# Opening stage of a two-block transformer kernel: normalization after the transposition, projections in one stage

## The chip, the core and the metric

The kernel runs on one core of a Trainium2 chip. The metric is the device time in microseconds of one execution. A core has five engines with their own instruction streams: TensorE (PE; PEld is its weight load), VectorE (DVE), ScalarE (ACT), GpSimd (POOL) and SyncE (SP), which here only issues DMAs. They meet through semaphores.

## What is computed

The reference is a block with a gated mixer (differential attention, banded attention) and a mixture of experts, followed by a second block. The change touches only its beginning:

```python
h = layer_norm(x, ln_in_g, ln_in_b)      # x: (1, 512, 1024); (x - mu) * rsqrt(var + 1e-5) * g + b
proj = h @ w_in
qa, ka, va = ...                         # the first three groups of 512 columns of proj
out_a = diff_attention(qa, ka, va, lam, lam_init, subln_w)   # 4 heads; p[0] - lam * p[1] of two softmaxes
...
h = layer_norm(DEEPNORM_ALPHA * h + m, ln1_g, ln1_b)         # the normalized h is needed again here
```

## The kernel before

`program` writes one core's streams stage by stage; a `Stage` ends when all engines have joined (the line of these joins is L80 in the profile). Matrices are multiplied as pairs of fp32r parts: an operand is split in an upper part (ScalarE casts it) and a lower part (`split_lower`, L141, raw minus upper), and `split_product` (L134 to L136) issues three matmuls: upper by upper, upper by lower, lower by upper. `k.x_parts` holds the transposed activations, eight chunks of 128 features by 512 rows. `k.ahead` is a buffer for weights that are loaded ahead (its lower part lies over it), `k.v_upper` that of their upper part.

The opening has three stages.

- `setup_stage` ("setup"): SyncE loads x in two halves (`x_in`), gain and shift spread to all partitions, the value weights (`load_ahead`, 2 MB), and stores two small rows of relative biases. ScalarE issues the constants and small loads, makes the four bias tables `alibi` (L354), and takes the root (L205). VectorE takes the statistics of the four row tiles (L118), the mean and variance (L199, L201), the inverse with one correction (L210 to L221), and normalizes each row tile in two passes: L227 ((x - mean) * gain) and L230 (times factor, plus shift), each 128x1024. TensorE only makes one small product (L365).
- `layer_norm_stage` ("ln0", with `done=NT`: rows are already normalized): SyncE writes the spread table `z_band` and loads the mask and the gain and shift of the next normalization; TensorE transposes x (L300: 32 of 128x128, four to a bank); ScalarE casts each chunk (L289), VectorE takes its lower part from the bank.
- `first_attention_stage` "diff" calls `heads_stage` (`early` is true: values are projected here). Unit u is one of four heads; its query and key weights lie in `raw0` for even u and over `k.ahead` for odd u. ScalarE casts the value weights (L789), VectorE splits them in four parts, TensorE projects values to banks 3 to 6, in groups of two chunks, once a part is split; then unit 0's queries and keys to banks 7 and 2 (`FIRST_PROJECTED`), with weights loaded from 35.87 (L867), cast (L761) and split on GpSimd. ScalarE copies queries (L783), VectorE keys (L810). From the first score (L454) on, `attention_pe` weaves the products of unit u + 1 (`projection`) between the steps of unit u. The second unit's weights can only be loaded when the value products have ended, since they lie over the value weights.

What sets the order is each engine's program order and its waits; there is no planner.

## Time and profile before

| what | us |
|---|---|
| median of 3 runs (lowest, highest) | 2136.57 (2133.35, 2140.83) |
| the profiled execution's own time | 2135.08 |
| its span in the trace | 2133.2 |
| TensorE busy in the span | 1939.7 (91%), 10052 matmuls |
| VectorE busy | 1602.6 (75%) |
| ScalarE busy | 1226.0 (57%) |
| GpSimd busy | 296.6 (14%) |

The page has the shares of the whole span. A busy share is a mean over stages with different limits, so the order of time within a stage is what tells what waits for what. Stretches are given from the start of the span. The granted clock (PEclk) is the share of TensorE's full 2.4 GHz; it has two levels, 1.00 and 0.50.

### The profile page before, as it was taken

What the parts mean: (1) busy time and instruction counts of PE and PEld (TensorE: products, weight loads), DVE (VectorE), ACT (ScalarE), POOL (GpSimd) and SP (SyncE); (2) the same over time, 40 slices, a digit from 0 to 9 for tenths busy, and PEclk for the clock granted to TensorE, in tenths of its full rate; (3) what the DMA queues carried; (4) which work ended last, traced back from release to release, by engine and by line L of the source; (5) the groups of instructions that cost most, each with busy time, mean ns of one, the idle gap of its engine ahead of it and who ended that gap; (6) DMA issues with size and microseconds to landing.
All of it is one profiled execution on the core that took longest, in us unless ns stands there. A gap on an engine that the chain in (4) does not pass through costs nothing. (4 is left out here: it accounts for less than half of the span.)

```text
span 2133.2 us, 28805 instructions
## 1 busy us (share of the span) xinstructions
PE 1939.7 (91%) x10052; PEld 1553.1 (73%) x10052; DVE 1602.6 (75%) x1819; ACT 1226.0 (57%) x1311; POOL 296.6 (14%) x172
## 2 busy tenths in 40 slices
PE   4988999974999999999999999999999388989998
PEld 3766678753788888888888888888888276576876
DVE  5362441457899999999999999999998544634786
ACT  3343532323677777777777777777777134643551
POOL 0202044101021212120212121211111000000000
PEclk9999999986999999999999999999999688999999
DMA  6222143445899999999999999999999362011122
GB/s 207 60 79 80 30 104 104 161 139 232 311 372 393 372 394 365 398 376 393 372 390 374 389 373 394 371 393 371 396 375 349 88 154 60 16 36 59 54 67 79
DMA packets 201613, 518.95 MB, mean 243 GB/s; under 512 B 21975, under 2 KB 81503, under 8 KB 201197
## 3 DMA queue, kind: packets, MB, share of 16 engines
q1 hardware_dynamic: 191212, 482.68, 60.9%
q0 software_dynamic: 9504, 34.61, 6.3%
q8 instruction: 41, 0.67, 0.1%
q10 hardware_dynamic: 832, 0.80, 0.1%
q14 instruction: 24, 0.19, 0.0%
HBM read 494.41 MB, written 29.41 MB: 246 GB/s over the span
## 5 line engine op out<-in xcount | busy, mean ns | idle before, releaser
L1770 ACT CAST moe_upper<-piece 128x2048 fp32r<-128x2048 f32 x384 | 734.2, 1914 | 282.5 <-PE bank L1702 268.0
L1850 DVE TENSOR_TENSOR piece_lower<-piece,moe_upper 128x2048 fp32r<-128x2048 f32 x384 | 870.2, 2286 | 28.4 <-ACT moe_upper L1770 28.4
L1700 PE MATMUL bank<-moe_upper,x_hi 128*128 128x512 f32 x1536 | 620.5, 404 | 2.5 <-DVE x_hi L1844 2.5
L1702 PE MATMUL bank<-moe_upper,x_hi 128*128 128x512 f32 x1536 | 605.8, 394 | 0.0
L1701 PE MATMUL bank<-piece_lower,x_hi 128*128 128x512 f32 x1536 | 601.2, 391 | 0.0
L1700 PEld LDWEIGHTS bank<-moe_upper,x_hi 128*128 128x128 f32 x1536 | 289.9, 189 | 67.8 <-DVE piece_lower L1850 2.9
L1701 PEld LDWEIGHTS bank<-piece_lower,x_hi 128*128 128x128 f32 x1536 | 290.1, 189 | 63.0
L1702 PEld LDWEIGHTS bank<-moe_upper,x_hi 128*128 128x128 f32 x1536 | 289.5, 188 | 62.8
L1654 POOL DMA_INDIRECT mixed<-moe_y,moe_dst x32 | 104.7, 3272 | 27.5 <-issue 27.5
L136 PE MATMUL bank<-x_hi,ahead_lower 128*128 128x512 f32 x256 | 102.0, 398 | 0.0
L1652 POOL COPY moe_dst<-row 128x1 uint32 (+1 forms) x32 | 7.0, 218 | 621.0 <-ACT moe_y L1759 621.0
L1644 POOL COPY moe_tok<-token 128x1 uint32 (+1 forms) x34 | 24.8, 729 | 335.1 <-DMA mixed<-moe_y,moe_dst 273.7
L1137 DVE TENSOR_TENSOR merge_tmp<-merge_sig,bank 128x512 f32<-128x512 f32 x8 | 5.5, 688 | 81.7 <-PE bank L136 81.4
L1646 POOL DMA_INDIRECT ahead<-h,moe_tok x34 | 61.7, 1813 | 32.5 <-issue 32.5
L300 PE MATMUL bank<-const,xs 128*128 128x128 f32 x96 | 18.0, 359 | 44.3 <-DVE xs L230 24.3
L136 PEld LDWEIGHTS bank<-x_hi,ahead_lower 128*128 128x128 f32 x256 | 49.4, 193 | 11.0
L135 PE MATMUL bank<-ahead_lower,x_hi 128*128 128x512 f32 (+1 forms) x140 | 55.4, 395 | 0.0
L134 PE MATMUL bank<-x_hi,merge_upper 128*128 128x512 f32 x128 | 50.4, 394 | 4.1 <-DVE ahead_lower L141 4.1
L1839 DVE TENSOR_TENSOR moe_a<-moe_u,moe_sg 128x512 f32<-128x512 f32 x64 | 44.3, 693 | 10.6 <-issue 10.2
L300 PEld LDWEIGHTS bank<-const,xs 128*128 128x128 f32 x96 | 15.8, 190 | 48.6 <-DVE xs L230 45.2
L135 PE MATMUL bank<-x_lo,merge_upper 128*128 128x512 f32 x128 | 50.5, 395 | 0.0
L1833 DVE SCALAR_TENSOR_TENSOR moe_u<-moe_u,moe_g 128x512 f32<-128x512 f32 x64 | 44.3, 693 | 5.9
(570 smaller groups left out, 3031.5 us busy)
## 6 DMA issues: line engine op xcount, KB each, us to landing
piece<-in_w_exp_in_dram SPq DMA_DIRECT2D x256, 1024.0 KB, 7.6
piece<-in_w_exp_out_dram SPq DMA_DIRECT2D x128, 1024.0 KB, 9.5
ahead<-in_w_in_dram SPq DMA_DIRECT2D x19, 512.0 KB, 4.1
ahead<-in_w_in_dram SPq DMA_DIRECT2D x3, 2048.0 KB, 9.3
ahead<-in_w_in_dram SPq DMA_DIRECT2D x4, 1536.0 KB, 7.0
merge_raw<-in_w_in_dram SPq DMA_DIRECT2D x8, 512.0 KB, 5.4
ahead<-in_w_out_dram SPq DMA_DIRECT2D x2, 2048.0 KB, 8.0
out_w<-in_w_out_dram SPq DMA_DIRECT2D x2, 2048.0 KB, 8.3
```

Source lines behind the costliest of these rows:

```text
L134: nc.tensor.matmul(out, lhs.hi, rhs.hi, start=start, stop=False)
L135: nc.tensor.matmul(out, lhs.hi, rhs.lo, start=False, stop=False)
L136: return nc.tensor.matmul(out, lhs.lo, rhs.hi, start=False, stop=stop)
L1646: nc.gpsimd.indirect_dma_start(out=rows_in[p][:, :], out_offset=None, in_=k.h1[:, :], in_offset=bass.IndirectOffsetOnAxis(ap=tok[:, p:p + ...
L1654: nc.gpsimd.indirect_dma_start(out=k.mixed[:, :], out_offset=bass.IndirectOffsetOnAxis(ap=dst[:, 0:1], axis=0), in_=y[:, :], in_offset=Non ...
L1700: nc.tensor.matmul(to, hi[:, f, :], upper[u][:, t, cols], start=f == 0 and not biased, stop=False)
L1701: nc.tensor.matmul(to, hi[:, f, :], lower[s][:, t, cols], start=False, stop=False)
L1702: done = nc.tensor.matmul(to, lo[:, f, :], upper[u][:, t, cols], start=False, stop=f == NK - 1)
L1770: nc.scalar.copy(upper[h % SPLIT][:, :, :], ring[s][:, :, :]).then_inc(hi_ready, 1)
L1833: nc.vector.scalar_tensor_tensor(out=u2[half][:, :], in0=u2[half][:, :], scalar=1.0, in1=g2[half][:, :], op0=ALU.add, op1=ALU.mult)
L1839: nc.vector.tensor_tensor(a2[half][:, :], u2[half][:, :], sg2[half][:, :], ALU.mult) .then_inc(a_ready, 1)
L1850: nc.vector.tensor_tensor(lower[s][:, :, :], ring[s][:, :, :], upper[h % SPLIT][:, :, :].bitcast(F32), ALU.subtract).then_inc(lo_ready, 1)
```

## The change

The three pieces (setup, first normalization, and value and first unit's projection) become one stage, `opening_stage`; `FirstNorm` and `setup_stage` go.

- x is loaded in four tiles. Gain and shift are also loaded as 16 rows of 128, transposed by one TensorE instruction and copied to `cols`, a column for each chunk.
- A row tile is only centered and scaled by its own factor: tiles 0 and 2 on VectorE (`tensor_scalar`), 1 and 3 on ScalarE (`Identity` with scale and offset). Gain and shift are applied after the transposition, where they are one number a partition, as VectorE takes the chunk from its bank to `full`, a ring of three; ScalarE then casts from `full`, VectorE subtracts.
- The split of the value weights is woven into this loop. TensorE turns chunks 0 to 3 (banks 0, 1, 2, 7), then alternates two chunks' value products with turning two further chunks, and adds unit 0's queries and keys. Unit 0's weights are loaded at the start of the program, and split on VectorE.
- The row tiles of x get gain and shift afterwards, in two passes each (`scaled_row`): three before VectorE waits for the value products, the fourth at the end.
- The second unit's weights are loaded, cast and split in this stage too, behind the value products (`v_ps`); the next normalization's gain and shift are loaded last (`scaled`, NT + 1). The write of `z_band` and the load of the mask stand ahead of these.
- The mask of `alibi` and the weight `neg_lam` are made on VectorE in the attention stage, behind the copy of the keys (`differential_weight`). `heads_stage` skips for units 0 and 1 what is done already (`opened`, `split`).
- The new stage's semaphores are kept and freed with those of the experts' stages.

```diff
-class FirstNorm:
...
-def setup_stage(nc, k, A, alibi):
...
+OPEN_TURNED, OPEN_VALUES = (0, 1, 2, 7), (3, 4, 5, 6)
+
+
+def opening_stage(nc, k, A, alibi, oa_first):
+
+    w_in = A["w_in"][0]
+    (raw, lower, upper), v_w = oa_first, Split(k.v_upper[:, :, :], k.ahead_lower[:, :, :])
+    unit_w = [Split(upper[:, NK * n:NK * n + NK, :], lower[:, NK * n:NK * n + NK, :]) for n in range(2)]
+    next_raw, next_lower, next_upper = second_unit(k, 2 * NK)
+    with Stage(nc, "setup", k.spent) as st:
...
         @block.sync
         def _(sp):
-            for h in range(2):
-                sp.dma_start(k.x[:, 2 * h:2 * h + 2, :], A["x"][0, 2 * h * P:2 * (h + 1) * P, :]
-                             .rearrange("(i p) n -> p i n", p=P)).then_inc(x_in[h], 16)
+            for i in range(NT):
+                sp.dma_start(k.x[:, i, :], A["x"][0, i * P:(i + 1) * P, :]).then_inc(x_in[i], 16)
+            for n, v in enumerate(("ln_in_g", "ln_in_b")):
+                sp.dma_start(rows_in[NK * n:NK * n + NK, :], A[v].rearrange("(c p) -> c p", p=P)).then_inc(rows_landed, 16)
+            for h in range(4):
+                sp.dma_start(k.ahead[:, 2 * h:2 * h + 2, :], column_tiles(w_in, 2 * WA, 512)[:, 2 * h:2 * h + 2, :])\
+                    .then_inc(v_in[h], 16)
+            for n in range(2):
+                sp.dma_start(raw[:, NK * n:NK * n + NK, :], column_tiles(w_in, n * WA)).then_inc(unit_in, 16)
             load_norm(sp, k, A["ln_in_g"], A["ln_in_b"])
-            for h in range(2):
-                sp.wait_ge(x_in[h], 16)
-            load_ahead(sp, k, column_tiles(A["w_in"][0], 2 * WA, 512))
             sp.wait_ge(band_ready, 1)
             sp.dma_start(k.band_row, band_row[:, :]).then_inc(k.row_stored, 16)
             sp.wait_ge(t5_ready, 1)
             sp.dma_start(k.t5_row, t5_row[:, :]).then_inc(k.row_stored, 16)
             sp.wait_ge(k.row_stored, 32)
+            spread_row(sp, k.z_band, k.band_row, k.band_stored)
+            sp.dma_start(k.hg_mask[:, :], A["c_mask"]).then_inc(k.mask_in, 16)
+            sp.wait_ge(v_ps, NT)
+            for n in range(2):
+                sp.dma_start(next_raw[:, NK * n:NK * n + NK, :], column_tiles(w_in, n * WA + P)).then_inc(next_in, 16)
+            sp.wait_ge(scaled, NT + 1)
+            load_norm(sp, k, A["ln1_g"][0], A["ln1_b"][0])
 
         @block.scalar
         def _(act):
-            act.dma_start(k.const[:, :], A["c_f32"]).then_inc(const_in, 16)
             act.dma_start(rb[:, :], A["rel_bias"][0]).then_inc(rb_in, 16)
             act.dma_start(onehot[:, :], A["c_onehot"]).then_inc(t5_in, 16)
             act.dma_start(table[:, :], A["rel_bias_2"]).then_inc(t5_in, 16)
+            act.dma_start(k.const[:, :], A["c_f32"]).then_inc(const_in, 16)
             for n, v in enumerate(("lambda_q1", "lambda_k1", "lambda_q2", "lambda_k2")):
                 act.dma_start(lv[:, n, :], row_broadcast(A[v][0])).then_inc(lam_in, 16)
-            act.wait_ge(const_in, 16)
+            act.wait_ge(t5_ps, 1)
+            nc.scalar.copy(t5_row[:, 0:512], k.bank[OPEN_VALUES[0]][0:6, :])
+            act.drain().then_inc(t5_ready, 1)
+            act.wait_ge(cols_ps, 1)
+            nc.scalar.copy(cols[:, :], k.bank[OPEN_VALUES[1]][:, 0:2 * NK]).then_inc(cols_ready, 1)
+
+            def values_upper(h):
+                act.wait_ge(v_in[h], 16)
+                part = slice(2 * h, 2 * h + 2)
+                nc.scalar.copy(k.v_upper[:, part, :], k.ahead[:, part, :]).then_inc(v_hi, 1)
+
+            act.wait_ge(var_ready, 1)
+            norm.deviation(0, NT).then_inc(std_ready, 1)
+            values_upper(0)
+            act.wait_ge(scaled, 1)
+            for i in (1, 3):
+                nc.scalar.activation(k.x[:, i, :], k.x[:, i, :], ACT.Identity, scale=norm.r[:, i:i + 1],
+                                     bias=offset[:, i:i + 1]).then_inc(normed, 1)
+            for c in range(NK):
+                act.wait_ge(taken, c + 1)
+                nc.scalar.copy(k.x_parts.hi[:, c, :], full[:, c % 3, :]).then_inc(hi_copied, 1)
+                if c % 2 == 0 and c < 6:
+                    values_upper(c // 2 + 1)
+            act.wait_ge(unit_in, 32)
+            for n in range(2):
+                part = slice(NK * n, NK * n + NK)
+                nc.scalar.copy(upper[:, part, :], raw[:, part, :]).then_inc(unit_hi, 1)
             for h in range(4):
                 nc.scalar.activation(alibi[:, h, :], k.const[:, C_DIST:C_DIST + S], ACT.Copy,
                                      scale=2.0 ** (-2 * (h + 1)))
-            act.wait_ge(t5_ps, 1)
-            nc.scalar.copy(t5_row[:, 0:512], k.bank[0][0:6, :])
-            act.drain().then_inc(t5_ready, 1)
-            act.wait_ge(var_ready, 1)
-            rows.deviation(0, NT).then_inc(std_ready, 1)
+            act.wait_ge(v_ps, NT)
+            for i in (0, 2):
+                nc.scalar.copy(k.v[:, i, :], k.bank[OPEN_VALUES[i]][:, :])
+            act.wait_ge(next_in, 32)
+            for n in range(2):
+                part = slice(NK * n, NK * n + NK)
+                nc.scalar.copy(next_upper[:, part, :], next_raw[:, part, :]).then_inc(next_hi, 1)
+            act.wait_ge(k.lam_ready, 1)
+            nc.scalar.activation(k.lam_exp[:, :], k.lam_sum[:, :], ACT.Exp)
 
         @block.tensor
         def _(pe):
             pe.wait_ge(t5_in, 32)
-            nc.tensor.matmul(k.bank[0][0:6, :], table[:, :], onehot[:, :], start=True, stop=True).then_inc(t5_ps, 1)
+            nc.tensor.matmul(k.bank[OPEN_VALUES[0]][0:6, :], table[:, :], onehot[:, :], start=True, stop=True)\
+                .then_inc(t5_ps, 1)
+            pe.wait_ge(const_in, 16)
+            pe.wait_ge(rows_landed, 32)
+            nc.tensor.transpose(k.bank[OPEN_VALUES[1]][:, 0:2 * NK], rows_in[:, :], k.ident[0:2 * NK, 0:2 * NK])\
+                .then_inc(cols_ps, 1)
+
+            def turn(c):
+                if c >= 4:
+                    pe.wait_ge(taken, c - 3)
+                for i in range(NT):
+                    last = nc.tensor.transpose(k.bank[OPEN_TURNED[c % 4]][:, i * P:(i + 1) * P],
+                                               k.x[:, i, c * P:(c + 1) * P], k.ident)
+                last.then_inc(transposed, 1)
+
+            pe.wait_ge(normed, NT)
+            for c in range(4):
+                turn(c)
+            pe.wait_ge(t5_ready, 1)
+            pe.wait_ge(cols_ready, 1)
+            for h in range(4):
+                pe.wait_ge(v_lo, h + 1)
+                for c in (2 * h, 2 * h + 1):
+                    pe.wait_ge(copied, c + 1)
+                    for i in range(NT):
+                        last = split_product(nc, k.bank[OPEN_VALUES[i]][:, :], k.x_parts[:, c, i * P:(i + 1) * P],
+                                             v_w[:, c, :], c == 0, c == NK - 1)
+                        if c == NK - 1:
+                            last.then_inc(v_ps, 1)
+                if h < 2:
+                    turn(4 + 2 * h)
+                    turn(5 + 2 * h)
+            for n in range(2):
+                pe.wait_ge(unit_lo, n + 1)
+                for c in range(NK):
+                    split_product(nc, k.bank[FIRST_PROJECTED[n]][:, :], unit_w[n][:, c, :], k.x_parts[:, c, :],
+                                  c == 0, c == NK - 1)
...
             for i in range(NT):
-                dve.wait_ge(x_in[i // 2], 16)
+                dve.wait_ge(x_in[i], 16)
                 statistics(nc, k, i)
             dve.drain()
-            rows.variance(dve, 0, NT).then_inc(var_ready, 1)
+            norm.variance(dve, 0, NT).then_inc(var_ready, 1)
             dve.wait_ge(std_ready, 1)
-            rows.inverse(dve, 0, NT)
-            dve.wait_ge(gain_in, 16)
-            dve.wait_ge(shift_in, 16)
-            for i in range(NT):
-                rows.row(dve, i).then_inc(normed, 1)
+            norm.inverse(dve, 0, NT)
+            nc.vector.scalar_tensor_tensor(out=offset[:, :], in0=norm.mv[:, :, 0], scalar=-1.0, in1=norm.r[:, :],
+                                           op0=ALU.mult, op1=ALU.mult).then_inc(scaled, 1)
+            for i in (0, 2):
+                nc.vector.tensor_scalar(k.x[:, i, :], k.x[:, i, :], norm.mv[:, i, 0:1], norm.r[:, i:i + 1],
+                                        ALU.subtract, ALU.mult).then_inc(normed, 1)
+            dve.wait_ge(cols_ready, 1)
+            for t in range(NK + 1):
+                if t < NK:
+                    dve.wait_ge(transposed, t + 1)
+                    if t >= 3:
+                        dve.wait_ge(copied, t - 2)
+                    nc.vector.tensor_scalar(full[:, t % 3, :], k.bank[OPEN_TURNED[t % 4]][:, :], cols[:, t:t + 1],
+                                            cols[:, NK + t:NK + t + 1], ALU.mult, ALU.add).then_inc(taken, 1)
+                if t % 2 == 0 and t < NK:
+                    part = slice(t, t + 2)
+                    dve.wait_ge(v_hi, t // 2 + 1)
+                    split_lower(nc.vector, k.ahead[:, part, :], k.v_upper[:, part, :],
+                                v_w.lo[:, part, :]).then_inc(v_lo, 1)
+                c = t - 1
+                if c >= 0:
+                    dve.wait_ge(hi_copied, c + 1)
+                    split_lower(nc.vector, full[:, c % 3, :], k.x_parts.hi[:, c, :], k.x_parts.lo[:, c, :])\
+                        .then_inc(copied, 1)
+            for n in range(2):
+                part = slice(NK * n, NK * n + NK)
+                dve.wait_ge(unit_hi, n + 1)
+                split_lower(nc.vector, raw[:, part, :], upper[:, part, :], lower[:, part, :]).then_inc(unit_lo, 1)
             dve.wait_ge(lam_in, 64)
             nc.vector.tensor_tensor(lp[:, 0, :], lv[:, 0, :], lv[:, 1, :], ALU.mult)
             nc.vector.tensor_tensor(lp[:, 1, :], lv[:, 2, :], lv[:, 3, :], ALU.mult)
             dve.drain()
-            nc.vector.tensor_reduce(k.lam_sum[:, :], lp[:, :, :], AX.X, ALU.add)
+            nc.vector.tensor_reduce(k.lam_sum[:, :], lp[:, :, :], AX.X, ALU.add).then_inc(k.lam_ready, 1)
+            dve.wait_ge(gain_in, 16)
+            dve.wait_ge(shift_in, 16)
+
+            def scaled_row(i):
+                nc.vector.tensor_tensor(k.x[:, i, :], k.x[:, i, :], k.gain[:, :], ALU.mult)
+                dve.drain()
+                nc.vector.tensor_tensor(k.x[:, i, :], k.x[:, i, :], k.shift[:, :], ALU.add).then_inc(scaled, 1)
+
+            for i in range(NT - 1):
+                scaled_row(i)
+            dve.wait_ge(v_ps, NT)
+            for i in (1, 3):
+                nc.vector.tensor_copy(k.v[:, i, :], k.bank[OPEN_VALUES[i]][:, :])
+            for n in range(2):
+                part = slice(NK * n, NK * n + NK)
+                dve.wait_ge(next_hi, n + 1)
+                split_lower(nc.vector, next_raw[:, part, :], next_upper[:, part, :], next_lower[:, part, :])
+            scaled_row(NT - 1)
+
+    k.norm.counted(normed=NT, std_ready=1)
+
+
+def second_unit(k, width):
+
+    return [x[:, 0:width // 4, :].rearrange("p a (b n) -> p (a b) n", n=P) for x in (k.ahead, k.ahead_lower, k.v_upper)]
+
+
+def differential_weight(nc, k, alibi, dve):
+
+    nc.vector.memset(alibi[0:HD, :, S - HD:S], NEG)
+    nc.vector.tensor_tensor(k.neg_lam[:, :], k.lam_exp[:, 1:2], k.lam_exp[:, 0:1], ALU.subtract)
+    dve.drain()
+    nc.vector.tensor_scalar(k.neg_lam[:, :], k.neg_lam[:, :], -LAM_INIT, None, ALU.add)
+    dve.drain()
...
+                opened=False, prepare=None):
+
+    early = values is not None and not projected_values and not opened
+    v_rows = range(2 if projected_values else 0, 0 if values is None or opened else NT)
...
+        split = 2 if opened else done
...
-            return k.bank[FIRST_BANK if u < done else FIRST_PROJECTED[n] if u == 0 else PROJECTED]
+            return k.bank[FIRST_BANK if u < done and keys is None else FIRST_PROJECTED[n] if u == 0 else PROJECTED]
...
-            for u in range(done, units):
+            for u in range(split, units):
...
+                if c == 0 and u >= split:
+                    pe.wait_ge(w_split, split0 + u * projections + n + 1)
...
-            if beside is None:
+            if beside is None and split < 2:
                 for n in range(projections):
                     upper_part(1, n)
...
+                if keys is not None and done <= u < units:
+                    dve.wait_ge(projected, projected0 + u * projections + projections)
                 if keys is not None and u < units:
-                    dve.wait_ge(projected, projected0 + u * projections + projections)
                     nc.vector.tensor_copy(keys[u % 2], place_of(u, 1)[:, :]).then_inc(evacuated, 1)
...
             next_keys(0)
+            if prepare is not None:
+                prepare(dve)
...
-                setup_stage(nc, k, A, table)
-                layer_norm_stage(nc, "ln0", k, k.x, x_t=k.x_parts, following=(A["ln1_g"][0], A["ln1_b"][0]),
-                                 first=FirstNorm(nc, k, A, table), done=NT)
+                (first_raw, first_lower), first_upper = overlaid(nc, s2, "first_raw", [P, 2 * NK, P]), s2.enter_context(
+                    nc.sbuf_tensor("first_upper", [P, 2 * NK, P], F32R))
+                first = first_raw, first_lower, first_upper
+                opening_stage(nc, k, A, table, first)
...
-                    lambda m: k.neg_lam[:, :] if m else None, differential_out, mixed=True, following=band_values)
+                    lambda m: k.neg_lam[:, :] if m else None, differential_out, mixed=True, following=band_values,
+                    first=first, opened=True, prepare=lambda dve: differential_weight(nc, k, table, dve))
```

## Rows read from the trace of the kernel before

**Rows 1.** Page, second part: busy tenths of TensorE in 40 slices

```profile
PE   4988999974999999999999999999999388989998
```

**Rows 2.** Stretches: length; PE, PEld, DVE, ACT, POOL busy (count); clock; DMA share, GB/s

```profile
27.00:31.00 4.00, 3.72 (x18) 3.75 (x19) 1.59 (x3) 3.17 (x6) 0.00 (x0) 1.00 0.69 246
31.00:33.00 2.00, 1.98 (x16) 1.61 (x14) 1.84 (x4) 1.94 (x4) 0.00 (x0) 1.00 1.02 256
33.00:36.00 3.00, 0.00 (x0) 0.00 (x0) 2.13 (x6) 0.76 (x3) 0.00 (x0) 1.00 0.90 273
...
38.20:41.40 3.20, 3.15 (x7) 2.51 (x8) 3.20 (x3) 1.58 (x2) 0.00 (x0) 0.50 1.04 386
41.40:61.60 20.20, 20.20 (x90) 16.73 (x89) 0.89 (x2) 3.17 (x4) 4.74 (x2) 1.00 0.16 39
```

**Rows 3.** Order of time, opening: start, us, engine, line, operation [idle before]

```profile
10.66 1.28 ACT L205 ACT_TABLE_LOAD   x1
11.23 2.47 DVE L118 BATCH_NORM_STATS2 stats<-xs 128x6 f32<-128x512 f32 x4 [0.86 <-DMA xs<-in_x_dram]
...
16.03 1.28 DVE L227 SCALAR_TENSOR_TENSOR xs<-xs,setup_mv,gain 128x1024 f32<-128x1024 f32 x1 [0.16 <-issue]
...
25.06 1.28 DVE L230 SCALAR_TENSOR_TENSOR xs<-xs,setup_r,shift 128x1024 f32<-128x1024 f32 x1
...
26.69 0.29 DVE L390 TENSOR_REDUCE lam_sum<-setup_lp 128x2 f32<-128x128 f32 x1
27.24 0.58 SPq L155 DMA_DIRECT2D z_band<-band_row  x1
```

**Rows 4.** Transpositions of the opening: in order of time, and by line (ns min/median/max)

```profile
27.28 5.70 PE L300 MATMUL bank<-const,xs 128*128 128x128 f32 x32 [17.32 <-PEq L80]
...
L300 PE MATMUL bank<-const,xs x32: 272/421/445, 27.3 to 32.7; 128*128 128x128 f32 x32
```

**Rows 5.** Order of time, from value products to first score

```profile
38.25 0.80 PE L134 MATMUL bank<-v_upper,x_hi 128*128 128x512 f32 x1 [5.27 <-DVE ahead_lower L141]
...
61.62 0.39 PE L134 MATMUL bank<-x_hi,diff_upper 128*128 128x512 f32 x1
...
72.70 0.69 DVE L810 COPY diff_heads_kt<-bank 128x512 f32<-128x512 f32 x1 [10.19 <-PE bank L136]
...
73.54 0.49 PE L454 MATMUL bank<-diff_heads_kt,diff_heads_q 64*128 64x128 f32 x4 [0.88 <-DVE diff_heads_kt L810]
```

**Rows 6.** Groups by line and shape: busy us, mean ns | idle before

```profile
L141 DVE TENSOR_TENSOR x_lo<-bank,x_hi 128x512 fp32r<-128x512 f32 x8 | 5.1, 687 | 2.6 <-ACT x_hi L289 2.6
L141 DVE TENSOR_TENSOR ahead_lower<-ahead,v_upper 128x1024 fp32r<-128x1024 f32 x4 | 4.6, 1220 | 1.8 <-ACT v_upper L789 1.8
L789 ACT CAST v_upper<-ahead 128x1024 fp32r<-128x1024 f32 x4 | 3.9, 1042 | 2.2 <-PEq L80 2.2
L1824 DVE TENSOR_SCALAR moe_g<-bank 128x512 f32<-128x512 f32 x64 | 41.0, 682 | 0.0
```

**Rows 7.** DMA: issues (KB each, median us to landing), then in order of time

```profile
z_band<-band_row SPq DMA_DIRECT2D x1, 2560.0 KB, 11.2
diff_raw<-in_w_in_dram SPq DMA_DIRECT2D x4, 512.0 KB, 6.5
ahead<-in_w_in_dram SPq DMA_DIRECT2D x2, 512.0 KB, 4.6
...
28.50 0.42 SPq L149 DMA_DIRECT2D gain<-in_ln_g_dram  x1
28.96 0.63 SPq L150 DMA_DIRECT2D shift<-in_ln_b_dram  x1
...
61.81 0.99 SPq L867 DMA_DIRECT2D ahead<-in_w_in_dram  x2
```

**Rows 8.** Stretches at the attention's end: length, TensorE busy (count), clock, DMA

```profile
133.61:137.02 3.41, 1.08 (x7) 1.00 0.00 0
137.02:140.44 3.42, 3.28 (x15) 0.50 0.02 5
```

More of the change, by code:

```diff
@@ L249, in _ @@
                 load_ahead(sp, k, ahead)
-            if first is not None:
-                first.spread(sp)
             if save is not None:
@@ L703, in _ @@
         def _(pool):
-            for u in range(done, units):
+            for u in range(split, units):
                 for n in range(projections):
```

64 lines of the change are left out of this document (24 added, 40 removed).

## The prediction

> **What bounds the kernel now.** I read the page first: TensorE is busy in nine tenths of the span, but the first of its 40 slices says 4 [rows 1]. The chain that ended last covers only the final few instructions, so it says nothing of the opening; I went on to the stretches (busy time and granted clock), then the order of time. The reader is to see a ladder in which each rung waits for the whole rung below. The statistics of the last two row tiles start at 11.23; the row scaling runs on VectorE alone from 16.03 to 26.34 (25.06 + 1.28); only after the stage joins at 27.24 does TensorE transpose, 27.28 to 32.98; then it stands 5.27 us until VectorE has split the first part of the value weights; the value products run 38.25 to 61.62, the first unit's 61.62 to 72.5, the keys are copied at 72.70, and the first score starts at 73.54 [rows 3 to 5]. In all of this TensorE's needed work is 5.7 + 23.4 + 10.9 = 40 us out of 73.5. Behind the first score the code of the change is the old one, and TensorE is full (every released unit has the next unit's products woven in). So the gain is the shift of the first score plus whatever clock is lost or won around it, and I price just that.
>
> **The change part by part.** Times are from the span's start.
>
> *Statistics.* Row tiles arrive one by one, in the same queue with the same bytes ahead of the last one, so the last lands near 11.2 as now; behind it stand two statistics instead of four. Four took 2.47 [rows 3], so they end at 12.5, not 13.7. From there to the first scaled row it takes 16.03 - 13.70 = 2.33 now. New on that way: ScalarE's copy of the gain and shift columns stands ahead of the root, with the small loads (queued behind x, about 11.6), one transposition (0.45), the copy (0.3) and then the root's table load of 1.28 [rows 3]: the root can't start before 13.6, 0.4 later than VectorE asks. Then the offset, 0.2: the factors are ready at 15.4.
>
> *Row scaling.* Eight VectorE passes of 1.28 leave the path; two rows stand on VectorE, two on ScalarE. For one ScalarE row the nearest is the 128x1024 cast, 1.04 [rows 6]: two end at 17.5. VectorE's two end there at the latest 0.5 later, if each costs a full 1.28. The function Identity has no row here: if it wanted a table load, 1.28 more; I take 0, since the casts after each of the loads in this opening needed none. The Trainium skill (ScalarE: Activation LUTs, section Table sets) says that identity sits in every set, which gives the same 0; no row shows it.
>
> *First product.* Turning chunk 0 is four transpositions. Those of now come at two speeds, 18 in 3.72 us and then 16 in 1.98 [rows 2]: 0.21 and 0.12 apart. Four at the slow pace and the end of the last: 18.5. VectorE then does in order the scaled eviction of chunk 0, the lower part of two value chunks, the eviction of chunk 1 and the lower part of chunk 0. An eviction with two factors has the row of 682, a lower part 687 for 512 columns and 1220 for 1024 [rows 6]; back to back each is some 0.07 shorter, so 3 x 0.62 + 1.16 and 0.2 of signalling: the first product starts at 21.8, now 38.25. Bounds: 20.9 (none of the small delays) to 24.0 (Identity load, VectorE rows at 1.28, 0.5 of later landing).
>
> *Value products.* The same 96 matmuls: 23.37 now, seven of them at half clock [rows 2, 5]. Woven in are the other 16 transpositions, 0.12 apart, 1.9, and 0.25 for the seams. VectorE has 2 x (0.62 + 0.62) + 1.16 = 3.6 us of work per pair of chunks where TensorE has 5.4 + 0.9, so it keeps up. The tight place is a wait: VectorE's eviction of chunk 4 waits for its turning, which TensorE does only after the first eight products' groups, and the lower part of chunk 3 is queued behind that eviction and a value split, 0.62 + 1.16 + 0.62 = 2.4 us, while TensorE has one more turning and chunk 2, 0.45 + 2.7: 0.7 of slack; the same again at chunks 5 and 6. Cost zero; if each VectorE step took 0.3 more, up to 0.5 in all. Products end at 21.8 + 23.4 + 1.9 + 0.25 = 47.3, now 61.62.
>
> *First unit.* Its weights land near 21; casts and splits (2 of 1.04, 2 of 1.22, on VectorE instead of GpSimd) end near 42, ahead of 47.3. Products 10.9, to 58.2. Hidden.
>
> *What ends the stage.* Now it is another chain. SyncE waits for the last value product, then loads the second unit: issue apart 0.5 and 4.6 to landing, 5.1 [rows 7]. ScalarE casts (1.04 to the first), VectorE splits two (after the first cast, 2.4), then the fourth row of x in two passes of 1.22, and SyncE, queued on that, issues two loads of 0.42 + 0.63 [rows 7]. 47.3 + 5.1 + 1.0 + 2.4 + 2.45 + 1.05 = 59.3. That is 1.1 behind TensorE. Joining the stage costs 0.26 (VectorE's last reduction ends 26.98, SyncE goes on at 27.24 [rows 3]) up to some 0.7: the keys are copied at 60.0 and the first score starts 0.84 later as now, at 60.85. The four tables, the lambda sums, three rows of x and the copies of the values lie in ScalarE's and VectorE's free time before 47.3 and during the second unit's load. The mask and lambda weight moved behind the keys copy take about 0.7 on VectorE and end as the first score is there. GpSimd's splits of two units go.
>
> *Sum.* 73.54 - 60.85 = 12.7 saved. *Clock.* TensorE then stands from 58.2 to 60.85. The granted clock stayed up over the 0.9 us at 72.6 and fell over 33 to 38; at the end of this same attention it fell to half after a stretch busy 1.08 of 3.4, whose longest stop was 2.0 [rows 2, 8]. 2.65 us is nearer to the rows that fell. A fall costs what the slow stretch at 38.2 cost, 7 x 0.2 and a part, 1.6, for the first unit's attention is full of woven products. I charge it: 11.1 saved.
>
> The profiled execution took 2135.08, which gives 2124.0; the median of the runs shown, 2136.57, lies 1.5 above it, and a median is what will be compared: **2125.5**.
>
> At the other end the rows speak of the clock too. 38.25 began slow after a stop; the first product at 21.8 follows 3.4 us of transpositions and a stop of 0.8. In the trace the clock rose under transpositions alone: they last from 272 to 445 ns with a median of 421, and the fast ones are the later [rows 2, 4]. So the 1.6 within 23.37 may go; I keep it, since the nearest row of a product behind a stop, 38.25, was slow. The Trainium skill (TensorE: Matmul & The Clock Gate, section Part 4: PE-mode transpose) says that transpositions don't count as work for the clock gate; the durations here speak against it. By the rule the slow start is certain, by the row it may be absent: 2125.5 or 2123.9.
>
> **The rivals.**
> *A, more is gained.* One of the two slow stretches is absent: 2125.5 - 1.6 = 2123.9; both: 2122.3. For it: the durations of the transpositions, and that 58.2 to 60.85 is half of the stop that surely cost. Against: the row at 137.
> *B, the entry and the exit are longer.* First product at the upper bound (+2.2) and the second unit's loads at the 6.5 of the first unit's row instead of 4.6 (+1.9) [rows 7]: 2125.5 + 4.1 = 2129.6. For it: 14 loads stand in SyncE's queue at once; against: in the trace loads landed in order of issue.
> *C, slower.* The clock stays at its lower level through both projections, because TensorE is fed in pieces: each product 0.427 instead of 0.227. With 137 products beyond the seven charged that is +27.4: 2153. It outweighs the gain from 56 such products on. For it: the tight hand-over at chunks 3 and 5; against: 3.6 of VectorE work to 6.3 of TensorE's per pair, so stops stay short.
> *D, no change.* The write of the spread table (2560 KB, 11.2 us [rows 7]) now stands ahead of the second unit's loads. If it is still moving at 47.3, they land up to 11.2 late and the stage ends that much later: 2136.7. It would have to be issued after 36; its small source rows are queued behind about 4.6 MB and I put its issue at 26.
>
> **How the numbers follow.** Forecast 0.45, A 0.30, B 0.15, C 0.05, D 0.05. The likeliest case is the forecast at 2125.5. The range is 2119.5 to 2131: A with both stretches and 3 us less for the spread of the runs (2133.35 to 2140.83), up to B and 1.4 more; it leaves out C and D and some of B. A measurement of this kernel can tell about 0.3%, 6.4 us, from no change, so faster means under 2130.2: forecast and A whole, B for the half, less a little for the spread, 0.82; the same 0.13; slower 0.05.
>
> **What would show it.** Per step: the first score near 60.9 (the sum), first value product near 21.8, last near 47.3 (feeding), root not before 13.6, no table load at the Identity rows, SyncE's last issues near 59 as the stage's end, clock rows of half near 22 to 25 and near 61 to 64. All later marks must stand the same distance from the first score as now; if not, the premise that only the opening moves is wrong. A first product later than 24 or a z-table write still open at 47 makes it B or D; halves of the clock through 22 to 58 make it C.

## The result, and the profile after

| | before | after |
|---|---|---|
| median of 6 runs (lowest, highest), us | 2136.99 (2133.35, 2140.83) | 2121.74 (2119.41, 2127.52) |
| profiled execution, span | 2133.2 | 2120.3 |
| its own time | 2135.08 | 2122.07 |

The ratio is 0.9929, 95% interval 0.9916 to 0.9943: 15.2 us faster by the medians (12.2 to 18.0 by the interval), 13.0 by the two profiled executions. The forecast was 2125.5.

TensorE's row in the page's 40 slices of the changed kernel, with the same columns as [rows 1]:

```profile
PE   7979899956999999999999999999999388989998
```

The first slice went from 4 to 7. Order of time of the changed kernel (start, us, engine, line, operation), the lines that answer to [rows 3 to 5]. First, the way to the first product:

```profile
10.26 1.29 DVE L118 BATCH_NORM_STATS2 stats<-xs 128x6 f32<-128x512 f32 x2 [1.38 <-DMA xs<-in_x_dram]
...
11.27 1.28 ACT L178 ACT_TABLE_LOAD   x1
12.56 0.20 ACT L178 ACTIVATE setup_std<-setup_ve 128x4 f32<-128x4 f32 x1
...
16.65 3.67 PE L396 MATMUL bank<-const,xs 128*128 128x128 f32 x16 [5.61 <-ACT xs L358]
21.29 0.76 PE L134 MATMUL bank<-v_upper,x_hi 128*128 128x512 f32 x1 [0.96 <-DVE x_lo L141]
```

Then the first unit's products, the last of them, SyncE's last loads, the copy of the keys and the first score:

```profile
46.84 0.39 PE L134 MATMUL bank<-x_hi,first_upper 128*128 128x512 f32 x1
...
57.49 0.39 PE L136 MATMUL bank<-x_hi,first_raw_lower 128*128 128x512 f32 x1
...
58.67 0.35 SPq L149 DMA_DIRECT2D gain<-in_ln_g_dram  x1
59.05 0.43 SPq L150 DMA_DIRECT2D shift<-in_ln_b_dram  x1
...
59.93 0.69 DVE L926 COPY diff_heads_kt<-bank 128x512 f32<-128x512 f32 x1 [1.29 <-PEq L80]
60.68 0.49 PE L567 MATMUL bank<-diff_heads_kt,diff_heads_q 64*128 64x128 f32 x4 [2.79 <-DVE diff_heads_kt L926]
```

The first score comes 73.54 - 60.68 = 12.86 earlier, and the span is 2133.2 - 2120.3 = 12.9 shorter: the whole difference of the two profiles stands before the first score. The first value product of the stage behind this attention has moved by the same 12.86 (before, then after):

```profile
146.46 0.79 PE L134 MATMUL bank<-v_upper,x_hi 128*128 128x512 f32 x1 [4.60 <-DVE ahead_lower L141]
```

```profile
133.60 0.79 PE L134 MATMUL bank<-v_upper,x_hi 128*128 128x512 f32 x1 [4.60 <-DVE ahead_lower L141]
```

If ScalarE's instructions of the two profiles are paired one by one, all from the first score to 150 stand 12.83 to 12.88 apart. Later the distance wanders between 12.0 and 15.0 and comes back to 13.0 at the end, so nothing lasting is won or lost there. Stretches of the opening, columns as in [rows 2]:

```profile
21.20:25.20 4.00, 3.91 (x9) 3.13 (x10) 3.71 (x5) 2.19 (x3) 0.00 (x0) 1.00 0.58 229
25.20:46.80 21.60, 21.60 (x104) 17.98 (x103) 14.49 (x19) 7.43 (x11) 0.00 (x0) 1.00 0.45 133
46.80:57.70 10.90, 10.90 (x49) 8.83 (x48) 8.92 (x10) 4.57 (x6) 0.00 (x0) 1.00 0.36 96
57.70:60.60 2.90, 0.18 (x1) 0.00 (x0) 1.61 (x2) 0.60 (x1) 0.00 (x0) 1.00 0.33 93
60.60:64.00 3.40, 3.32 (x16) 2.48 (x16) 0.96 (x8) 0.88 (x4) 0.00 (x0) 1.00 0.95 292
```

TensorE is full from 21.29 to 57.7: the ladder has become one woven stretch. The nine products in the first 4.0 us are slow ones. The granted clock reads 1.00 there only because its records in this trace begin at the first change, near 25.2; nine in 4.0 is 0.43 to 0.44 apiece, the pace of the 0.50 row in [rows 2]. The last two rows show what was charged and didn't come: TensorE stood 3.0 us, and behind it 16 matmuls went in 3.4 us at full clock.

### The profile page after: what moved, and what is told of

Same layout as the page of the kernel before. It is cut to its first block and busy times, and to the rows that moved or that the text cites. A ratio compares the mean times of both kernels' runs of the same rounds, so it can differ in the third digit from the quotient of the medians.

```text
span 2120.3 us, 28827 instructions
## 1 busy us (share of the span) xinstructions
PE 1940.5 (92%) x10053; PEld 1553.8 (73%) x10053; DVE 1614.4 (76%) x1834; ACT 1228.8 (58%) x1314; POOL 290.7 (14%) x168
## 5 line engine op out<-in xcount | busy, mean ns | idle before, releaser
L1763 POOL COPY moe_tok<-token 128x1 uint32 (+1 forms) x34 | 33.6, 988 | 333.6 <-DMA mixed<-moe_y,moe_dst 273.1
L1765 POOL DMA_INDIRECT ahead<-h,moe_tok x34 | 56.6, 1664 | 33.0 <-issue 33.0
L1958 DVE TENSOR_TENSOR moe_a<-moe_u,moe_sg 128x512 f32<-128x512 f32 x64 | 44.3, 693 | 10.6 <-issue 10.2
L1878 ACT ACTIVATE moe_y<-bank,slot_weight 128x512 f32<-128x512 f32 x64 | 40.2, 680 | 15.1 <-PE bank L1821 15.1
L1929 DVE TENSOR_TENSOR x_hi<-bank,x_hi 128x512 fp32r<-128x512 f32 x66 | 42.4, 683 | 8.3 <-ACT x_hi L1871 8.2
```

Of the source, the lines that this page charges most:

```text
L1765: nc.gpsimd.indirect_dma_start(out=rows_in[p][:, :], out_offset=None, in_=k.h1[:, :], in_offset=bass.IndirectOffsetOnAxis(ap=tok[:, p:p + ...
L1958: nc.vector.tensor_tensor(a2[half][:, :], u2[half][:, :], sg2[half][:, :], ALU.mult) .then_inc(a_ready, 1)
```

## The experiments

All are edits of the changed kernel. What each profile showed, in us from the span's start (first product of the values, first product of unit 0, first score, and the granted clock at half between unit 0's first product and 90):

| kernel | values | unit 0 | score | half clock | span |
|---|---|---|---|---|---|
| before | 38.25 | 61.62 | 73.54 | none | 2133.2 |
| after | 21.29 | 46.84 | 60.68 | none | 2120.3 |
| after, again (e11) | 21.23 | 47.13 | 61.08 | none | 2121.4 |
| e1, rows first | 29.89 | 55.87 | 67.95 | none | 2129.7 |
| e2, second unit later | 21.56 | 47.23 | 59.31 | 63.3 to 73.6 | 2133.8 |
| e7, turned first | 25.28 | 48.40 | 62.16 | 62.0 to 65.5 | 2123.0 |
| e6, longer exit | 21.26 | 47.11 | 63.92 | 63.4 to 70.2 | 2128.0 |
| e3, idle work at the entry | 20.80 | 46.09 | 59.98 | none | 2116.9 |
| e4, more of it | 21.15 | 44.87 | 58.76 | 58.3 to 65.2 | 2123.5 |
| e5, fourth row early | 21.86 | 47.76 | 59.84 | none | 2122.4 |
| e8, x in halves | 22.28 | 45.95 | 59.74 | 59.4 to 66.2 | 2121.3 |
| e10, exit filled | 21.62 | 45.34 | 59.42 | none | 2116.1 |
| e9, filled and early | 21.17 | 44.90 | 58.77 | none | 2120.6 |
| e12, tail filled too | 21.38 | 45.10 | 58.98 | none | 2118.9 |

e3 to e8 were run once each, so they have no median and no interval; they are read by their marks. A span alone misleads here. Paired ScalarE instructions show that e3 and e10 stand 0.5 and 1.2 ahead of the changed kernel at 1700 us and 3.8 and 4.8 ahead at 2000, far behind anything that was edited.

### e1: the rows get gain and shift before the transposition

```diff
-            for i in (0, 2):
-                nc.vector.tensor_scalar(... ALU.subtract, ALU.mult).then_inc(normed, 1)
+            dve.wait_ge(gain_in, 16)
+            dve.wait_ge(shift_in, 16)
+            for i in range(NT):
+                norm.row(dve, i).then_inc(normed, 1)
...
-                    nc.vector.tensor_scalar(full[...], ..., cols[:, t:t + 1], ..., ALU.mult, ALU.add)
+                    nc.vector.tensor_copy(full[:, t % 3, :], k.bank[OPEN_TURNED[t % 4]][:, :])
```

ScalarE's two rows and the late `scaled_row` passes go too, and the loads of the spread gain and shift rows move up, right behind x.

> Undoes one part: the rows of x are normalized with gain and shift before the transposition again, in eight VectorE passes of 1.28, and the gain and shift rows are loaded right behind x; the stage, the early loads and the weaving stay. Ladder theory (the changed kernel's first product at 21.3 and first score at 60.7 are ends of one chain): the transpositions start where eight passes end, 14.0 + 10.3 = 24.3 instead of 16.6, so first product near 29 (7.7 later); the exit is shorter by some 2, as the rows of x are out of it and TensorE ends the stage: first score near 66.4, the kernel about 5.7 us slower than the changed one. Rival (merging the stages and the early loads make the gain, since TensorE then bounds the opening and a late start is caught up): first score within 1 us of 60.7.

Measured: ratio to the kernel before 0.9966 (0.9952 to 0.998), median 2130.91: 9.2 slower than the changed kernel's median, 5.7 of the gain left. The way to the transpositions:

```profile
15.14 1.28 DVE L200 SCALAR_TENSOR_TENSOR xs<-xs,setup_mv,gain 128x1024 f32<-128x1024 f32 x1 [1.35 <-DMA shift<-in_ln_in_b_dram]
...
24.16 1.28 DVE L203 SCALAR_TENSOR_TENSOR xs<-xs,setup_r,shift 128x1024 f32<-128x1024 f32 x1
25.50 3.68 PE L392 MATMUL bank<-const,xs 128*128 128x128 f32 x16 [14.61 <-DVE xs L203]
```

The rows start 1.35 late, as the spread shift row lands at 15.1, and end 8.85 after the changed kernel's; the first score is 7.3 later, as the ladder has it, the exit being 1.8 shorter (unit 0's first product to first score 12.08 against 13.84). The expectation had 5.7, with the rows starting at once and an exit shorter by 2. A late start is not caught up, so the rival fell. The span is 9.4 longer, not 7.3: 2.5 more go at the end of the attention, where this profile has 17.1 us at half clock (123.5 to 126.9 and 133.7 to 147.4) and the changed kernel's 10.2 (below, e12).

### e2: the second unit's weights are prepared in the attention stage

```diff
-            sp.wait_ge(v_ps, NT)
-            for n in range(2):
-                sp.dma_start(next_raw[...], column_tiles(w_in, n * WA + P)).then_inc(next_in, 16)
...
-        split = 2 if opened else done
+        split = done
```

> Undoes another part: the second unit's weights are loaded, cast and split (on GpSimd) in the attention stage, as before the change. Theory that the exit chain (load 5.7, cast, split, fourth row, SyncE's loads) costs only what it reaches beyond TensorE's first unit: the stage ends about 1 us earlier, so first score near 59.5, but then the first unit's attention has to wait for weights: loaded from 58.6, landed 63.5, cast 65.6, split on GpSimd from 64.6 to 67 and 69.4, while TensorE wants them at 60: it stands about 7 us. In all 5 to 6 us slower than the changed kernel. Rival (the exit chain is a mere burden, weights are hidden in the attention): 1 us faster than the changed kernel.

Measured: ratio 0.9972 (0.9962 to 0.9982), median 2131.95, 10.2 slower than the changed kernel. What TensorE waited for before 130 (us in total, times, longest), and the stretch:

```profile
PE bank L134 <- POOL ahead_lower L141: 8.1, 1, 8.1
...
63.30:73.60 10.30, 5.73 (x14) 4.12 (x16) 0.00 (x0) 2.77 (x6) 4.67 (x2) 0.50 0.44 105
```

The first score comes 1.4 earlier (the expectation had 1), and then TensorE stands 8.1 for GpSimd's part, whose chain starts with a load issued at 58.5. The expectation had 7 and no word of the clock, which falls in the stop. Behind the half clock the same ScalarE instructions are 9.3 later than in the changed kernel: 8.1 - 1.4 from the stop, 2.6 from the clock. Another 1.3 go at the attention's end. (The profiled execution was the slowest of its nine, 3.65 above their median, so its span in the table is too long to compare.) So the longer exit is bought: 1.4 us of it spares 10.

### e7: all eight chunks turned before the first value product

```diff
-            for c in range(4):
+            for c in range(NK):
                 turn(c)
...
-                if h < 2:
-                    turn(4 + 2 * h)
-                    turn(5 + 2 * h)
```

> Undoes the weaving: all eight chunks are turned before the first value product. Theory (TensorE bounds the woven stretch, VectorE has 3.9 us of work per pair of chunks to TensorE's 6.3): the first product waits until VectorE has evicted chunks 4 to 7's predecessors, at about 25.0 instead of 21.3, but no transposition stands between products any more (1.9 less): last value product near 48 to 49, 1 to 2 later; first score near 62. Rival (the hand-over at chunks 3 and 5 holds TensorE up, so weaving costs as much as it hides): last value product at 47 or earlier.

First product 25.28, last before 48.40, first score 62.16: as expected. Weaving is worth 4.0 at the first product and only 1.5 at the first score, since TensorE takes the transpositions with it. The span was 2.7 longer: a fall of the clock at 62.0, which the changed kernel's profile doesn't have, added 1.5 more (ScalarE's instructions behind it are 2.9 later).

### e6: the exit chain 2.8 longer

```diff
+            for _ in range(4):
+                nc.vector.tensor_tensor(full[:, 0, :], full[:, 1, :], full[:, 2, :], ALU.add)
+                dve.drain()
             scaled_row(NT - 1)
```

> Doubles one suspected cost: four idle additions of 128x512 on VectorE (0.69 each, 2.8 together) ahead of the fourth row of x, nothing else. Theory (VectorE's last passes and SyncE's loads behind them end the stage, and TensorE's stop before the first score costs clock once it is long): first score at 60.7 + 2.8 = 63.5, TensorE stands 5.8 instead of 3.0, the granted clock falls for about 3.4 us and the first unit loses 1.6 more: span 4.4 us longer than the changed kernel's 2120.3. Rival (the stage ends with something else, or the stop doesn't move the clock): 0, or 2.8 alone.

Unit 0's first product to the first score: 16.81 against 13.84, 3.0 more; VectorE's last passes and SyncE behind them do end the stage. Then:

```profile
58.00:63.90 5.90, 0.15 (x1) 0.00 (x0) 4.39 (x6) 0.60 (x1) 0.00 (x0) 0.96 0.18 42
63.90:70.20 6.30, 6.28 (x18) 4.44 (x18) 0.91 (x7) 0.88 (x4) 0.00 (x0) 0.50 1.03 292
```

18 matmuls in 6.3 us, where the changed kernel has 16 in 3.4. The half clock lasted 6.8, not 3.4, and set the first unit back by 2.8 (the first score is 3.2 later than in the changed kernel, the ScalarE instructions behind the stretch 6.1). A fall there cost 2.8, not the 1.6 that I had charged. The span is 7.7 longer, where the expectation had 4.4; another 1.2 went at the attention's end.

### e3 and e4: idle transpositions on TensorE before the real ones, and before the first product

Both have the first loop; the second is e4's alone.

```diff
+            for _ in range(24):
+                nc.tensor.transpose(k.bank[OPEN_TURNED[3]][:, 0:P], k.ident, k.ident)
             pe.wait_ge(normed, NT)
...
+            for _ in range(16):
+                nc.tensor.transpose(k.bank[OPEN_VALUES[3]][:, 0:P], k.ident, k.ident)
```

> Adds 24 idle transpositions of the identity on TensorE (into a bank whose contents are overwritten later) while it waits for the scaled rows, from 11 to about 16.2. Theory (the nine value products at half clock are the price of the stop before them, and transpositions raise the clock): the granted clock is full before the real transpositions start at 16.6, chunk 0 is turned 0.4 earlier, and, if the clock holds over the stop before the first product (now 1.4, then about 3), the products lose 1.8 less: unit's products start near 44.8 instead of 46.8; if the stop drops the clock, only 0.4 is left. By the rule that transpositions don't count for the clock: nothing changes, 46.8.

> As the run before, with 16 more idle transpositions between the turning of chunk 3 and the first product, so that TensorE stands less than 1.5 there. Theory: no product of the opening is at half clock; products start near 20.9, the unit's products near 44.6, first score near 58.5, span 2.2 shorter than the changed kernel's 2120.3. By the rule that transpositions don't count: unit's products at 46.8 or later.

Stretches of e3 (two) and then of e4 (three):

```profile
10.90:14.20 3.30, 3.30 (x17) 3.26 (x17) 2.07 (x13) 2.72 (x5) 0.00 (x0) 1.00 0.67 207
...
21.10:24.50 3.40, 3.40 (x9) 2.67 (x8) 3.33 (x5) 2.19 (x3) 0.00 (x0) 0.50 0.71 276
```

```profile
16.90:20.50 3.60, 3.54 (x32) 3.47 (x32) 2.76 (x4) 1.64 (x4) 0.00 (x0) 1.00 1.16 320
21.10:44.80 23.70, 23.65 (x112) 19.75 (x113) 18.14 (x24) 9.63 (x14) 0.00 (x0) 1.00 0.47 166
...
58.70:65.20 6.50, 6.44 (x18) 4.60 (x20) 0.95 (x8) 0.88 (x4) 0.00 (x0) 0.50 0.99 283
```

In e3 the clock was up at 14.2 after 3.3 us of idle transpositions, and the real ones went at the fast pace. TensorE then stood 2.2 before the first product at 20.80, and the clock fell at 21.1: 0.7 won at the first score, the second case of the expectation (which had 0.4). In e4 it held, and the 96 products and 16 transpositions took 23.7 instead of 25.55: the slow start costs 1.85. So transpositions alone raise and hold the clock; the rule of the Trainium skill that they don't count (TensorE: Matmul & The Clock Gate, Part 4: PE-mode transpose) is not borne out. But e4's span is 3.2 longer than the changed kernel's though its first score is 1.9 earlier: the clock fell at 58.3, which cost 2.9, another 1.3 went at the attention's end, and the rest later. The expectation of a span 2.2 shorter failed.

### e5: the fourth row behind the third; e8: x in two halves

In e5 the last `scaled_row` behind the loop goes; in e8 x is loaded as two transfers of two tiles each, not four of one tile.

```diff
-            for i in range(NT - 1):
+            for i in range(NT):
                 scaled_row(i)
```

> Moves one step: VectorE scales the fourth row of x right behind the third, ahead of the copies of the values, so that nothing but the second unit's split stands behind its load. Theory (the exit is a chain of load, cast, split, row, SyncE's loads): VectorE is done at 56.2 and SyncE at 54, TensorE's last product of the unit at 57.7 ends the stage; first score near 59.0 instead of 60.7, span 1.7 shorter if the clock around it stays as it is. Rival (the stage's end is set by the second unit's load whatever stands behind it): first score still later than 60.

From unit 0's first product to the first score 12.08 instead of 13.84: 1.76, as expected; TensorE's stop is 1.2 instead of 3.0. The start happened to be 0.6 later. The span is 2.1 longer, not 1.7 shorter: 2.5 were lost between 115 and 130 (below, e12).

> Changes one size back: x is loaded in two halves instead of four tiles. Theory (only the last tile's two statistics follow the last landing): with halves four statistics follow it, so the turning starts 1.2 later, 17.9 instead of 16.6, and the first score near 61.9. Rival (the root's table load on ScalarE, ended 12.55 while VectorE's variance was ready at 12.30, hides it): 0.9 or less.

The turning starts at 17.64, 1.0 later, between the two expectations. The first score is 0.9 earlier nevertheless: in this execution the clock was up before the first product (its first matmul takes 0.47 instead of 0.76) and the products took 23.67. At this size the clock's luck covers the edit. The fall before the first score then cost 2.9.

### e11, e10, e9, e12: the changed kernel again, and TensorE's stops filled

e10 fills the exit (15 idle transpositions behind unit 0's products, 8 behind the join of the stages); e9 has this (with 14 for the 15), e4's and e5's edits; e12 adds idle transpositions in the last unit of the first attention, behind the attention and ahead of the next stage's value products.

```diff
+            for _ in range(15):
+                nc.tensor.transpose(k.bank[OPEN_TURNED[0]][:, 0:P], k.ident, k.ident)
...
+            if prepare is not None:
+                for _ in range(8):
+                    nc.tensor.transpose(k.bank[TURNED[0]][:, 0:P], k.ident, k.ident)
             attention_pe(nc, pe, k, items, b, projection, opened)
```

> The changed kernel once more, unchanged, beside the next two. Theory (the granted clock at the stop before the first score falls in some executions and not in others, worth 2.6 when it does, and this is in the spread of 2119 to 2128): runs spread over some 5 to 8 us around 2122, ratio to the kernel before 0.993 as the first time; the first score again at 60.7 plus or minus 0.6.

> Adds to the changed kernel only 15 idle transpositions behind the first unit's products and 8 behind the stage's join, so that TensorE stands about 1 instead of 3.0 before the first score. Theory (a stop there of 3 is at the edge: it dropped the clock in four of the six profiles of variants that have it and are not longer, each time for 2.6 us of the first unit): first score unchanged at 60.7, the clock never falls there, spread smaller, median 1 to 2 below the changed kernel's. By the rule that transpositions don't count: the clock falls as often as without.

> All that helped together: idle transpositions before the real ones, before the first product and around the join, and the fourth row of x early. Theory: first value product 20.9, unit's products 44.7, VectorE's last split (not SyncE's loads) ends the stage at 57.0, first score 58.4; clock full throughout; 2.3 less than the changed kernel's first score and no fall at it: median 2 to 4 below the changed kernel's, 2118 to 2120. Rival (clock falls elsewhere take it back): no difference that three decimals of a ratio show.

> The run with the filled opening and the early fourth row, and beside it idle transpositions in TensorE's stops at the end of the first attention: 10 before each wait for a normalized item of the last unit, 5 before each wait for a copied one, 14 behind the attention and 20 ahead of the next stage's value products. Theory (what the opening won was given back by half clock in 113 to 138, where TensorE stops for 2.0 and 4.6 in that profile): no half clock from the first score to 140, the stages behind the attention 2 to 3 us earlier than in the filled opening alone, median 2 to 3 below its 2121.6. Rival (these stages wait for VectorE, not for TensorE, so the clock there costs nothing, and idle transpositions only get in the way): median the same or up to 1 above.

(The expectation of e10 counts four falls in six profiles. Five profiles had been taken that have this stop at this length, and the clock fell in three of them: e4, e7 and e8.)

| kernel | median (lowest, highest) | ratio to before | 95% interval |
|---|---|---|---|
| e11, after again | 2123.23 (2118.16, 2125.02) | 0.9931 | 0.9915 to 0.9946 |
| e10 | 2121.44 (2117.9, 2123.33) | 0.9929 | 0.9913 to 0.9945 |
| e9 | 2121.61 (2120.28, 2122.83) | 0.9927 | 0.9913 to 0.9941 |
| e12 | 2121.78 (2115.49, 2122.07) | 0.9924 | 0.9911 to 0.9938 |

None can be told from the changed kernel, so the gains in the median that were expected of e10 (1 to 2) and e9 (2 to 4) were not seen. e10's first score, expected at 60.7, came at 59.42, and not by its edit: the clock was up before its first product, as in e8 (its value stretch took 23.72). In their profiles the steps do what was expected: in e9 TensorE is busy through the join, the first score is 1.9 earlier and the clock stays up behind it:

```profile
55.80:58.70 2.90, 2.60 (x23) 2.29 (x21) 0.93 (x3) 0.60 (x1) 0.00 (x0) 1.00 0.24 96
58.70:65.00 6.30, 6.30 (x32) 4.62 (x31) 2.27 (x15) 0.88 (x4) 0.00 (x0) 1.00 0.64 166
```

Then 1.3 of the 1.9 are gone by 130, and the span is 0.3 longer than the changed kernel's. e12 tried whether the half clock there took them; e9 first (two rows), then e12 (two rows):

```profile
113.60:117.00 3.40, 3.40 (x16) 2.52 (x16) 2.37 (x10) 2.04 (x9) 0.00 (x0) 0.50 0.70 264
...
113.00:133.00 20.00, 12.52 (x67) 9.15 (x65) 13.61 (x37) 10.89 (x26) 0.00 (x0) 0.77 0.25 80
```

```profile
115.00:118.40 3.40, 3.40 (x14) 2.27 (x13) 1.23 (x8) 1.57 (x5) 0.00 (x0) 0.50 0.34 124
...
113.00:131.00 18.00, 17.67 (x130) 14.87 (x130) 10.28 (x37) 7.30 (x23) 0.00 (x0) 0.91 0.18 70
```

In e12 the clock is up but for 115.0 to 118.4, and that is just the stretch that matters: e12 loses 1.6 there. Its 14 idle transpositions behind the attention also hold up the join. They end at 131.3, and VectorE starts on the next stage at 131.59, where e9's starts at 129.48. Most of this is made good by 145; from 600 to 1500 e12 is 0.8 behind e9. So the rival held for the time, and the filling did not remove the fall that cost something.

The other profiles show where the loss is. Paired ScalarE instructions, set against the changed kernel's, sort the thirteen other profiles (that of the kernel before too) in two groups. In eight (e1, e2, e4, e5, e6, e8, e9, e12) there is a stretch of 3.4 at half clock which, on the changed kernel's time, starts between 115.3 and 116.7, and each of them loses 1.2 to 1.6 between the instruction at 116.3 and the one at 119.0. In e9 TensorE is busy in all of these 3.4 us. In the other five (before, e3, e7, e10, e11) and in the changed kernel the first half-clock stretch behind 90 starts at 124.0 to 124.5 on that time, and they lose nothing (under 0.05). e1 and e5 lose another 1.1 by 130; they alone stay at half clock right through the next stretch (13.7 us), where the changed kernel has 3.4 at full clock. So the 2.5 of e1 and e5 and most of e9's 1.3 go with the clock's falls. Why it falls at the one place in some executions and at the other in the rest no run shows: the length of the opening does not sort them.

## Why the prediction was right

Its range held the time, and the first score, the mark on which it rests, was forecast at 60.85 and came at 60.68. The forecast was still 3.8 above the measured median (2125.5 against 2121.74), and that has two parts. 1.9 is in the profiled execution (2124.0 against 2122.07), nearly all of it the 1.6 charged for the clock. The other 1.8 is the median: it was put 1.5 above the profiled execution, as before the change, and came out 0.3 below it. Step by step:

- **Statistics and root.** Forecast 15.4 for the factors, measured 14.1. The last tile's statistics began at 10.26, not 11.2, and the root's table load, which I let end at 13.6, ended at 12.55, as the small rows landed before 10.8. Both sizes were off the same way.
- **Row scaling.** Two ScalarE rows at 1.04 forecast, 1232 ns each measured; turning began at 16.65, a little before the 17.5. No table load stands at the Identity rows. The 0.19 beyond the cast is what the Trainium skill gives for two operands of one number a partition, some 93 ns each (ScalarE: Activation LUTs, What ACT_TABLE_LOAD costs).
- **To the first product.** Forecast 4.3 from the last scaled row, measured 4.7: the eviction with two column operands takes 805 ns, not the 682 of its nearest row (two of them stand on this way, 0.2 in all), and the first began 0.2 later behind the turning than forecast. 21.29 against 21.8 is a sum of errors of 0.9 and 0.4 the other way.
- **Feeding.** 25.55 for the value stretch against 25.5. TensorE's list of waits has none between the first product and 57.7, so the hand-over at chunks 3 and 5 cost nothing, as said; rivals C and D fell with this (SyncE issued the spread table's write at 24.8; it landed 11.3 later, at 36).
- **Exit.** 13.55 forecast from unit 0's first product to the first score, 13.84 measured: the second unit's load took 5.7, not 5.1. e6 and e5 confirm the chain, e2 that it must be there.
- **The clock.** The step that failed. The 1.6 charged for a fall behind 58.2 didn't come in this profile, nor in e11 or e3; without it the working gives 2122.4 for the profiled execution, which took 2122.07. And where it fell it cost 2.8 to 2.9 (e4, e6, e8) or 1.5 (e7): the term was mis-sized too. This was rival A with one of its two stretches absent, 2123.9; the other, the slow products at the start, was there. That the median came nearer to A's 2122.3 for both is the part of the median above.
- **Behind the first score.** The premise that only the opening moves held: the next stage's first product stands 72.92 behind the first score in both profiles.
- **The median.** It fell by 15.2, the profiles differ by 13.0. The changed kernel's second set of runs has 2123.23, 13.3 below the median of its own neighbours (2136.53), so the distance of the two sets is the spread, and no further cause is needed.
- **Which part gives how much.** With the rows first (e1) 5.7 of the 15.2 are left; with the second unit later (e2) 4.7. The two don't add up (9.2 and 10.2 of 15.2), since each undoes a rung on which the others stand. What the joins between the stages and the early loads give by themselves no run tested.

## What to carry to other kernels

Where stages form a ladder and one busy engine follows, price the change by the one mark at which the old code resumes, and check that the shift is carried to the end unchanged. Scaling that is one number per row can be split from scaling that is one number per column and applied where it costs one pass instead of two; and a step may well be moved ahead into a stage that it lengthens (1.4 here) if its chain of load, cast and split would otherwise be waited for (8.1). Single profiles of variants that differ by less than about 3 us say nothing of the time here: read the marks, and time the kernel in several rounds. And before time is shaved off one stage, pair the instructions behind it: e9's first score came 1.9 earlier, and the clock took 1.2 of that back 55 us later.

## What was not expected of the hardware

Stops of the same length had different ends. Before the first score TensorE stood about 3 us in six profiles. In three of them the clock stayed up (idle before the first score by the timeline: after 2.79, e11 2.91, e3 2.85), in three it fell, for 3.4 to 6.8 us (e4 2.85, e7 2.72, e8 2.75). The longest stop kept it and the shortest lost it, so the length doesn't tell. The start is like that too: behind the same 16 transpositions the first products were slow in after, e11, e1, e2, e5 and e6, and fast in e8 and e10. From e8:

```profile
56.80:59.70 2.90, 0.19 (x1) 0.00 (x0) 1.61 (x3) 0.60 (x1) 0.00 (x0) 0.95 0.36 83
59.70:66.20 6.50, 6.46 (x18) 4.62 (x20) 0.93 (x7) 0.88 (x4) 0.00 (x0) 0.50 1.00 284
```

SyncE's issues took long while many loads were under way: of its loads at the start, two of 512 KB in rows of 512 bytes took 9.55 us to issue and the next 3.15, against 1 us for the same two at 59.89. The two small stores behind them went out at 18.75 and 19.12, where the kernel before had them at 11.71 and 12.29; nothing on the way to the first score waited for them.

```profile
5.48 9.55 SPq L319 DMA_DIRECT2D first_raw<-in_w_in_dram  x2
15.07 3.15 SPq L149 DMA_DIRECT2D gain<-in_ln_in_g_dram  x1
```
